# A two-block transformer kernel: short group of feed-forward chunks first, attention outputs copied out of their bank, context tokens loaded later, function table asked for ahead

## The reference

```python
# block 1, for each of two layers l
h = rms_norm(x, g_norm1) * (1 + sc1) + sh1
# two attentions over h @ w_in, merged ...
x = x + gt1 * (merged @ w_out)
h = rms_norm(x, g_norm2) * (1 + sc2) + sh2
x = x + gt2 * ((silu(a) * v) @ w_down)      # a, v: causal convolution of h @ w_up

# block 2, layer 0: convolution module, on x and on ctx; layer 1: attention, x over x and ctx
hx = rmsnorm(x, g0) * (1 + sc_x) + sh_x ;  hc = rmsnorm(ctx, g0) * (1 + sc_c) + sh_c
y  = (silu(layernorm(depthwise_conv(a * sigmoid(gt)))) ) @ w_pw2 + b_pw2         # layer 0
y  = softmax(q k^T / 8) v @ wo        # layer 1: 16 heads of 64, 512 queries, 768 keys
x  = x + g_x * rmsnorm(y, g1)         # and ctx in layer 0
f  = rmsnorm(x, g2) * (1 + scf) + shf
x  = x + gf_x * rmsnorm((silu(f @ w1) * (f @ w3)) @ w2, g3)   # D_FF_2 = 2816, and ctx in layer 0
# each sh, sc, g is a slice of silu(c) @ w_mod + b_mod
```

## Time and profile before

| | us |
|---|---|
| median of 3 executions | 3503.28 |
| lowest, highest | 3501.05, 3506.01 |
| the profiled execution, its own time | 3505.28 |
| its span in the trace | 3503.3 |
| PE busy in the span | 3318.2 (95%) |
| PE idle in the span | about 185 |

### The profile page before, as it was taken

One profiled execution on the slowest core, in us unless ns is written; L12 is line 12 of the kernel. 1 busy time (PEld: TensorE's weight loads), 2 busy tenths in 40 slices (PEclk: granted clock), 3 DMA queues, 4 the chain that ended last, 5 costly groups with the idle time before them and its releaser, 6 DMA issues.

```text
span 3503.3 us, 39850 instructions
## 1 busy us (share of the span) xinstructions
PE 3318.2 (95%) x16184; PEld 2543.0 (73%) x16184; DVE 1503.4 (43%) x2191; ACT 1195.1 (34%) x1758; POOL 761.9 (22%) x395
## 2 busy tenths in 40 slices
PE   7989999999998998999999899999998979999998
PEld 4657767777665775777777478888885758868886
DVE  3562133132365113313288654232336688653234
ACT  3433234233343223423331243211113456542222
POOL 4302434443330332333411000000000048400000
PEclk9999999999999999999999999999999989999999
DMA  6403434544430454455335211222210200023322
GB/s 227 135 21 96 145 111 140 164 139 154 122 109 0 139 162 135 154 186 160 117 98 123 50 49 57 64 62 65 67 52 22 61 25 1 25 67 90 103 87 69
DMA packets 431977, 337.28 MB, mean 96 GB/s; under 512 B 20766, under 2 KB 413304, under 8 KB 419509
## 3 DMA queue, kind: packets, MB, share of 16 engines
q1 hardware_dynamic: 430352, 334.23, 31.5%
q0 software_dynamic: 1248, 0.46, 0.1%
q10 hardware_dynamic: 196, 0.07, 0.0%
HBM read 319.58 MB, written 2.10 MB: 92 GB/s over the span
## 4 chain that ended last, share of the span: by engine, by line
PE 75%; DVE 7%; issue 2%; ACT 2%; SPq 0%; DMA 0%; DVEq 0%; ACTq 0%
PE PS L422 21%; PE PS L424 20%; PE PS L423 20%; PE PS L578 2%; PE PS L509 2%; PE PS L728 1%; PE PS L557 1%; PE PS L1028 1%; PE PS L995 1%; DVE both_tmp L1256 1%; PE PS L1030 1%; PE PS L1029 1%; PE PS L1006 1%; PE PS L883 1%; DVE tmp L1256 1%
## 5 line engine op out<-in xcount | busy, mean ns | idle before, releaser
L422 PE MATMUL PS<-Hh,Wh 128*128 128x512 f32 x2224 | 886.1, 398 | 20.8 <-DVE Hl L1270 14.6
L423 PE MATMUL PS<-Hl,Wh 128*128 128x512 f32 x2224 | 870.3, 391 | 0.0
L424 PE MATMUL PS<-Hh,Wl 128*128 128x512 f32 x2224 | 869.7, 391 | 0.0
L2286 POOL TENSOR_TENSOR Wl<-raw,Wh 128x1024 fp32r<-128x1024 f32 (+2 forms) x254 | 568.9, 2244 | 1163.6 <-ACT Wh L1848 1163.6
L1848 ACT ACTIVATE Wh<-raw 128x1024 fp32r<-128x1024 f32 (+3 forms) x444 | 437.5, 986 | 406.3 <-PE PS L424 397.9
L422 PEld LDWEIGHTS PS<-Hh,Wh 128*128 128x128 f32 x2224 | 420.4, 189 | 146.8 <-issue 81.3
L424 PEld LDWEIGHTS PS<-Hh,Wl 128*128 128x128 f32 x2224 | 420.0, 189 | 88.8
L423 PEld LDWEIGHTS PS<-Hl,Wh 128*128 128x128 f32 x2224 | 420.6, 189 | 68.2 <-issue 3.7
L1179 DVE TENSOR_TENSOR Wl<-raw,Wh 128x1024 fp32r<-128x1024 f32 (+3 forms) x190 | 219.8, 1157 | 394.8 <-ACT Wh L1848 394.4
L1754 DVE SCALAR_TENSOR_TENSOR cv<-PS,vcols,cv 128x510 f32<-128x510 f32 (+1 forms) x176 | 123.7, 744 | 299.2 <-ACT cv L2212 299.2
L422 PE MATMUL PS<-g_h,Wh 128*128 128x512 f32 x528 | 210.8, 399 | 0.7 <-DVE g_l L1308 0.6
(11 more groups left out here) (353 smaller groups left out, 5019.3 us busy)
## 6 DMA issues: line engine op xcount, KB each, us to landing
raw<-in_ffn_w SPq DMA_DIRECT2D x108, 512.0 KB, 3.7
mod_w<-in_w_mod SPq DMA_DIRECT2D x48, 1024.0 KB, 5.1
raw<-in_w_up SPq DMA_DIRECT2D x88, 512.0 KB, 3.8
mod_w<-in_w_ada SPq DMA_DIRECT2D x40, 1024.0 KB, 6.2
raw<-in_w_in SPq DMA_DIRECT2D x62, 512.0 KB, 4.0
UQ<-U SPq DMA_DIRECT2D x128, 99.4 KB, 2.2
raw<-in_w_down SPq DMA_DIRECT2D x32, 384.0 KB, 3.3
raw<-in_conv_w_pw SPq DMA_DIRECT2D x24, 512.0 KB, 4.3
```

The costliest lines, as they stand in the source:

```text
L422: pe.matmul(o, wh, xh, start=start, stop=False, skip_group_check=True)
L423: pe.matmul(o, wh, xl, start=False, stop=False, skip_group_check=True)
L424: return pe.matmul(o, wl, xh, start=False, stop=stop, skip_group_check=True)
L2286: pool.tensor_tensor(low, src, high.bitcast(F32), ALU.subtract).then_inc(*mark("w_low_pool", one[0]))
```

## The change

It does the following:

- `F_GROUPS` becomes (0, 2), (2, 6), ... (18, 22): the group of two chunks is first and not last.
- Where DVE adds squares up, it now adds those of chunk j - 1 ahead of the addition of job j, not behind it (both residual adds of block 1, both feed forwards of block 2).
- `ln_and_exp()`, which loads the function table if another one is in, stands ahead of the wait in `root`, and also ahead of the square of chunk 6.
- `keep_warm` follows the statistics listed in `WARM_AFTER`. For ("ln"), ("f", 0) and ("n", 1) that is now the one of ctx, with four matmuls; elsewhere it is unchanged (eight matmuls, after x).
- In the layer norm ACT takes the roots of x and of ctx behind all squares of both.
- The outputs of pw2 and wo2 are squared from their bank, ahead of the copy that frees it.
- ACT copies bank 7 into a new tile `y2_out` in SBUF, which frees the bank; `y2_h` and `y2_l` are then made from `y2_out`. That is one more ACT instruction for each of 16 heads. `y2_l` now has two inputs in SBUF. PE waits for `y2_low` ahead of wo2.
- ctx is loaded at ("up", 1, 1, 3), later than at ("up", 1, 0, 1).

```diff
@@ -260,7 +260,7 @@
     WQ = [at(f"WQ{i}", 44 + 3 * i, [QUADS, 4, 32]) for i in range(2)]
-    F_GROUPS = [(lo, min(lo + 4, FC)) for lo in range(0, FC, 4)]
+    F_GROUPS = [(max(0, hi - 4), hi) for hi in range(FC - 4 * (FC // 4), FC + 1, 4) if hi > 0]
     gb_h, gb_l = at("gb_h", 0, [4, BOTH], F32R), at("gb_l", 12, [4, BOTH], F32R)
@@ -273,6 +273,7 @@
     p2 += [at(f"p2{i}", 74 + 3 * (i - 2), [SEQ + CTX]) for i in (2, 3)]
+    y2_out = nc.alloc_sbuf_tensor_at("y2_out", [P, SEQ], F32, offset=int(tmp_base + 3 * KB))
     p2.append(nc.alloc_sbuf_tensor_at("p24", [P, SEQ + CTX], F32, offset=int(tmp_base)))
@@ -537,13 +538,18 @@
                 stat(("ss", tag), [((tag, c), 0, P, c == 0, c == KD - 1)], n)
-            if c == KD - 1 and stream(("ss", tag)) == "x":
-                keep_warm()
+            if c == KD - 1 and tag in WARM_AFTER:
+                keep_warm(WARM_AFTER[tag])
 
...
                 norm_stat(one, c, NS[s])
+
+        WARM_AFTER = {**{(n, l): WARM for n in ("n1", "n2") for l in range(DEPTH)}, ("n", 0, "x"): WARM,
+                      ("ln", "c"): 4, ("f", 0, "c"): 4, ("n", 1, "c"): 4, ("f", 1, "x"): WARM,
+                      **{("post", (y, l, "x")): WARM for y, l in (("ffn", 0), ("ffn", 1))},
+                      ("post", ("conv", "x")): WARM, ("post", ("att", "x")): WARM}
 
...
@@ -1042,7 +1048,7 @@
                 if j == 0:
-                    pe.wait_ge(*free(("y2", G_HEADS - 1)))
+                    pe.wait_ge(*ready("y2_low", G_HEADS - 1))
                 gemm(job, w, y2_h, y2_l, SEQ).then_inc(*fill(job))
@@ -1427,18 +1433,18 @@
                     dve.wait_ge(*ready("g_high", "both", f))
-                    low_of(gb_l[:, f % 4, :], gb_h[:, f % 4, :], i, BOTH, "g_low", "both", f)
+                    low_of(gb_l[:, f - lo, :], gb_h[:, f - lo, :], i, BOTH, "g_low", "both", f)
                 for j in range(KD):
...
                         ahead((*job, "w"))
+                    if hi == FC:
+                        for s in ("x", "c"):
+                            sum_squares(("post", ("ffn", 0, s)), j - 1)
                     if lo > 0:
...
                         dve.tensor_tensor(YB[:, j, :], YB[:, j, :], bank(job, BOTH), ALU.add).then_inc(*empty(job))
-                    if hi == FC:
-                        for s in ("x", "c"):
-                            sum_squares(("post", ("ffn", 0, s)), j - 1)
             post_norms(("ffn", 0), 0, 9)
@@ -1461,10 +1467,10 @@
                     if half == 1:
+                        sum_squares(("post", ("ffn", l, s)), j - 1)
                         dve.wait_ge(*full(job))
...
                         dve.tensor_tensor(Y[:, j, 0:n], Y[:, j, 0:n], bank(job, n), ALU.add).then_inc(*empty(job))
-                        sum_squares(("post", ("ffn", l, s)), j - 1)
             post_norm(("ffn", l, s), n, Y, lambda c: col(2, l, s, 9, c))
@@ -1731,8 +1737,8 @@
                 ahead(("wo", l, j))
+                sum_squares(("n2", l), j - 1)
                 add_to_x(("wo", l, j), col(1, l, "x", 2, j), j)
-                sum_squares(("n2", l), j - 1)
             dve.wait_ge(*free(("wo", l, KD - 1)))
@@ -1769,9 +1775,9 @@
                     ahead((*job, 1))
-                    add_to_x(job, col(1, l, "x", 5, j), j)
                     if half == 1:
                         sum_squares(("n1", 1) if l == 0 else ("n", 0, "x"), j - 1)
+                    add_to_x(job, col(1, l, "x", 5, j), j)
                 dve.wait_ge(*free(job))
@@ -1812,8 +1818,8 @@
                 dve.wait_ge(*ready("y2_high", h))
-                dve.tensor_tensor(y2_l[rows, h // 2, :], bank(("y2", h))[rows, :], y2_h[rows, h // 2, :].bitcast(F32),
-                                  ALU.subtract).then_inc(*empty(("y2", h)))
+                dve.tensor_tensor(y2_l[rows, h // 2, :], y2_out[rows, :], y2_h[rows, h // 2, :].bitcast(F32),
+                                  ALU.subtract).then_inc(*mark("y2_low", h))
         for j in range(KD):
@@ -1867,28 +1873,30 @@
 
-        def square(event, src, n, rows=slice(0, P)):
+        def square(event, src, n, rows=slice(0, P), bias=0.0):
+            if event[1] == KD - 2 and ("ss", event[0]) in sums_over:
+                ln_and_exp()
             if event[0] in SUMMED and event[1] == 0:
...
                     act.wait_ge(*sums_over[job][1])
-                act.activation(STATS[stream(job)][0][:, 0:n], src, ACT.Square).then_inc(*mark("squares", event))
+                act.activation(STATS[stream(job)][0][:, 0:n], src, ACT.Square, bias=bias).then_inc(*mark("squares", event))
                 return
...
                 act.wait_ge(*tally.square_free[tally.squares[i - 2]]())
-            act.activation(SQ[i % 2][rows, 0:n], src, ACT.Square).then_inc(*mark("squares", event))
+            act.activation(SQ[i % 2][rows, 0:n], src, ACT.Square, bias=bias).then_inc(*mark("squares", event))
             sq_n[0] += 1
...
             y = STATS[stream(job)][1]
+            ln_and_exp()
             act.wait_ge(*full(job))
...
                 act.wait_ge(*newton)
-            ln_and_exp()
             act.activation(y[:, 0:n], bank(job, n), ACT.Ln, scale=1.0 / count, bias=const("eps"))\
@@ -1953,9 +1962,10 @@
                 ahead(job)
+                act.wait_ge(*full(job))
+                for x, lo, hi in (("x", 0, SEQ), ("c", SEQ, BOTH)):
+                    square((("post", ("conv", x)), j), bank(job, BOTH)[:, lo:hi], hi - lo, bias=vec("b_pw2", j))
                 evict(job, YB[:, j, :], BOTH, ACT.Identity, vec("b_pw2", j))
-                act.wait_ge(*free(job))
-                squares_of_y(("conv",), j)
             for s in ("x", "c"):
...
@@ -2260,12 +2270,16 @@
                 act.wait_ge(*full(("y2", h)))
-                act.activation(y2_h[rows, h // 2, :], bank(("y2", h))[rows, :], ACT.Copy).then_inc(*mark("y2_high", h))
+                if h >= 2:
+                    act.wait_ge(*ready("y2_low", h - 2))
+                act.activation(y2_out[rows, :], bank(("y2", h))[rows, :], ACT.Copy).then_inc(*empty(("y2", h)))
+                act.wait_ge(*free(("y2", h)))
+                act.activation(y2_h[rows, h // 2, :], y2_out[rows, :], ACT.Copy).then_inc(*mark("y2_high", h))
         for j in range(KD):
             ahead(("wo2", j))
+            act.wait_ge(*full(("wo2", j)))
+            square((("post", ("att", "x")), j), bank(("wo2", j)), SEQ)
             evict(("wo2", j), Y2[:, j, :], SEQ)
-            act.wait_ge(*free(("wo2", j)))
-            square((("post", ("att", "x")), j), Y2[:, j, :], SEQ)
         root(("ss", ("post", ("att", "x"))), SEQ)
@@ -2380,7 +2394,7 @@
                   .then_inc(*mark("mod_w_in", block_of, r, by=16))
-            if key == ("up", DEPTH - 1, 0, 1):
+            if key == ("up", DEPTH - 1, 1, 3):
                 sp.wait_ge(*full(("wo", DEPTH - 1, KD - 1)))
...
```

More of the change, by code:

```diff
@@ L653, in ffn_both @@
                             pe.wait_ge(*ready("g_low", "both", f))
-                        g = [(x[:, f % 4, 0:SEQ], x[:, f % 4, SEQ:]) for x in (gb_h, gb_l)]
+                        g = [(x[:, f - lo, 0:SEQ], x[:, f - lo, SEQ:]) for x in (gb_h, gb_l)]
                         mm = both(job, w, f - lo, slice(j % 2 * P, (j % 2 + 1) * P), (g[0][0], g[1][0]), (g[0][1], g[1][1]),
@@ L1978, in ffn_both @@
                     if f == lo and lo > 0:
-                        act.wait_ge(*full(("dn_both", lo - 4, KD - 1)))
-                    high_of(gb_h[:, f % 4, :], ("g", f), BOTH, "g_high", "both", f)
+                        act.wait_ge(*full(("dn_both", F_GROUPS[F_GROUPS.index((lo, hi)) - 1][0], KD - 1)))
+                    high_of(gb_h[:, f - lo, :], ("g", f), BOTH, "g_high", "both", f)
                 for j in range(KD):
```

2 lines of the change are left out of this document (1 added, 1 removed).

## The result

| | before | with the change |
|---|---|---|
| median, us | 3502.8 | 3443.9 |
| lowest to highest of 4 | 3501.1 to 3506.0 | 3443.7 to 3444.4 |
| ratio, with its 95% interval | 1 | 0.9831 (0.9814 to 0.9848) |
| profiled execution, span, us | 3503.3 | 3441.8 |

A forecast was written before the change was run, and what follows sets the result against it. PE, busy 3318.2 of 3503.3 us, bounds the kernel. Terms 8.9 + 1.3 + 11.5 + 3.9 + 5.0 + 2.4 + 9.0 - 1.0 + 0.6 - 1.5 = 40.1 us gave a 3463 us median, range 3444 to 3480.

The forecast's parts named there:

- Step 7: Attention: PE's wait for the bank goes, but POOL's scaling delays DVE's subtraction 1.54 us a head; net -1.0 us.
- rival B: Attention: the subtraction isn't blocked, so +15.5 us in place of -1.0, 3447; chance 0.15.
- point 3: PE's restart after three inner norms: shorter idle time, no half clock behind it; 3.9 us, bounds 0 and 4.4.
- point 6: End of both streams' feed forward and ("n", 1): short group first, DVE keeps up, full clock, table, order; 9.0 us.
- step 8: Rest: squares from the bank behind wo2 save 0.6 us; possible half clock in ("f", 0) and ("n", 1) costs 1.5.
- steps 5: ("f", 0): ctx's statistic no longer stands behind 7.03 us of constants, so PE restarts 2.4 us earlier.
- 1. Sums and table: Sums before additions (0.94) and early table load (1.28): 8.9 us at four norms, 1.3 at ("n", 0).
- 2. Context: Norm ("n2", 1): later context load removes PE's 9.7 us wait for modulation weights and 1.8 of half clock; 11.5 us.
- 4. Layer norm: Layer norm: all squares in a row and constants behind ctx's statistic let PE restart 5.0 us earlier.
- C: Norms: half clock at new idle times and behind the restarts takes 13 us back, 3476; chance 0.14.
- D: End of the feed forward: DVE stays late, so 5.0 us of gain is lost, 3468; chance 0.05.
- E: Attention: every blocked subtraction falls wholly on PE, 24.6 us lost in place of 1.0, 3487; chance 0.06.

The follow-up runs named there:

- c_pool_two_inputs: The changed kernel, but POOL scales with a product of two tensors instead of tensor by scalar: 3453.6 us, ratio 0.9856.
- b: The kernel before, with only the new handling of the attention outputs (ACT's copy to SBUF frees the bank): 3487.8 us, ratio 0.9956.
- e_ctx_alone: The kernel before, with only the context's load moved later: 3489.0 us, ratio 0.9955.
- k: The changed kernel, with DVE's sums of squares behind the additions again: 3452.2 us, ratio 0.9852.
- h: The changed kernel, with the table load behind the wait in `root` and none ahead of chunk 6's square: 3451.1 us, ratio 0.9848.
- f: The changed kernel, with the old `F_GROUPS`, the short group last: 3458.7 us, ratio 0.9868.
- i: The changed kernel, with matmuls of constants moved into PE's idle time at the norms: 3447.3 us, ratio 0.9837.
- l: The changed kernel, with a POOL copy in place of its scaling: 3444.8 us.
- m: The changed kernel, with POOL scaling by the constant 0.5 instead of the reciprocal: 3443.9 us.

## Why the prediction was wrong

**Step 7 failed, and it alone is large.** It said that POOL's scaling would block DVE's subtraction until 0.55 us behind POOL's end. The mechanism exists: the earlier trace rows show it for a cast, and c_pool_two_inputs for a product of two tensors, to the hundredth. But the row was of another POOL instruction than the one in the attention, and the prediction said so ("has no row of the scaling") and then took the cast's price nonetheless. Measured, the tensor by scalar instruction holds DVE for its first part only: the subtraction ends 1.44 us behind POOL's start and takes 0.92 to 1.15 us in place of 0.68, not 2.2. The term that was mis-sized is the block, 0.24 to 0.47 us a head and not 1.54. The bank's wait went, with the price that the bounds had: +15.5 there, 15.1 by the traces, 15.7 by the medians. That is rival B's number, but not quite its mechanism, since B said that the subtraction isn't blocked.

The rest of the step stands. By c a head loses what DVE loses. With the forecast block, some 1.2 us longer than in after, a head would take about 11.1 us (an estimate: 9.87 and 1.2), 10.95 in before. That is the loss of about nothing that step 7 had.

The Trainium skill ("SBUF — State Buffer", section "Who interferes with whom") says that a DVE instruction with two SBUF inputs contends with a GpSimd (POOL) instruction that reads SBUF, and that the second of the two is blocked for the whole instruction of the first. The first half holds here for all four kinds, the second for copy, cast and product, and not for the scaling.

**The range** ended at 3444, three below rival B's 3447: 0.5 for point 3 and 2.4 for point 6. From B's 3446.7, the traces take off 0.8 (step 6), 1.5 (step 8, which did not come on top of steps 5 and 6) and 1.3 (ahead of the attention), and add 1.0, 0.7 and 0.4 (layer norm, "f", attention): 3445.2. The remaining 1.3 to 3443.9 need no further cause: by b and e the profile of before was 3.3 us too long ahead of the attention, and the sum took only 2.0 off its profiled execution. That the measured time lies so close to the range's edge is chance; before's own executions lie 5 us apart.

Point by point, by the stretches of the first table:

1. Sums and table: right at the norms it names. From the last product to the restart ("n2", 0) takes 10.9 us for 13.0, 2.1 less for 2.2 forecast, and ("n1", 1) the same. The 1.3 at ("n", 0) is 1.2, by the order alone (k); the table costs nothing there (h). That h's sum of 6 x 1.28 came out is luck: only four places pay.
2. Context: right in place and kind; the 9.7 is gone, the 1.8 too. Alone (e) it gave more, for the clock behind the restart.
3. Restarts: right, full clock behind all three, idle 1.38 us.
4. Layer norm: 4.0 for 5.0. Behind the four constants PE idles another 3.7 us for DVE, where it idled 5.5 in before. The half clock behind the restart isn't the cause: it falls in the next stretch, and before had it too, for 4.6 us behind its restart, after for 3.4. Which step of the chain I had 1.0 too short is not shown.
5. ("f", 0): 1.7 for 2.4, and only 0.85 of it in the norm (21.43 us from the last product to the restart, 22.28 in before); most of the rest is the clock behind the layer norm's restart. Here step 8's fear came true: idle 2.78 us ahead of the statistic, 3.4 us at half clock behind it, 6.04 us where 4.82 had been. The sum of steps 5 and 8 is near, in part by luck.
6. The short group: 9.8 for 9.0, and f shows that the group's size does it. The parts differ: 7.6 lie behind the last product and 2.2 ahead of it, the table's 1.3 and the order's 0.9 were not there (h and k move this stretch by 0.2 and 0.1), and the group's size gave more than its 6.8. In both traces PE runs 7 us of constants behind the statistic of x and, after that of ctx, idles the same 1.62 us for ACT, so a root that is ready earlier gained nothing.
7. Wrong, above.
8. The clock's risk, counted half at 1.5, came at both places: 3.4 us at half clock in ("f", 0) and in ("n", 1), 1.7 each, inside the gains of 1.7 and 9.8. The squares from the bank (0.6) were not run alone. The stretch from wo2 to the next restart is 0.66 shorter, but in six runs that leave it unchanged (c, f, i, k, l, m) it is 1.5 longer than in after, so this shows nothing.

Of the rivals, C came true in part (new half clock at "f" and "n" 1, 3.4 us in all), inside steps that gained more than they lost; D, E and F did not.

## What to carry to other kernels

Before a row of one instruction is used as the price of another, look whether the kind is the same: here cast, product and scaling on POOL all read SBUF, and the third holds DVE for less than half of its own time. To tell a short block from none, compare ends and not durations: an instruction that is held ends at a fixed distance from the other's start or end, whenever it began. An accumulation bank should be given free by one plain copy on the engine that reads it first; that was worth 15.7 us here, where ACT and DVE had held it one after the other, about as much as moving the context's load (16). And where an engine gets less per step (a short group) its partners may become the bound: put the short group where they have the least to do.

## What the runs showed of the hardware that I had not expected

- POOL's `tensor_scalar` on 128 x 768 takes 2.21 us, its `tensor_tensor` 1.47 and its copy 0.83. The longest of them holds DVE's two-input instruction little more than the shortest: it takes 0.92 to 1.15 us beside the first, 1.48 to 1.59 beside the product and 0.81 to 0.93 beside the copy (0.68 alone).
- The same instructions in the stretch ahead of the attention took 173.1 and 169.9 us in two kernels that do not differ up to there, with a mean granted clock of 0.89 and 0.91. A single profile is worth no more than 3 us there.
- Idle times of 2.66 us ahead of a restart had half clock behind them in before and none in e_ctx_alone at the same norm.
